# MoE outputs weighted as they leave PSUM and summed in DRAM by an accumulating scatter, instead of stored as pairs and summed at the end

## The reference, cut to what matters

```python
x = x + concat([y_ssd, y_hgrn]) @ w_out            # the residual rows
h = rmsnorm(x, norm_ffn_w)
p_group = softmax(h @ router_group)                # 4 groups, the best one is taken
g_w = max(p_group)
top_w, top_i = top_k(softmax(logits of that group), 2)   # 2 of its 4 experts
top_w = top_w / sum(top_w)
c = g_w * top_w                                    # two gates for each token
for each of 16 experts e:                          # D 1024, expert width 256
    hid = silu(h @ w_gate[e]) * (h @ w_up[e])
    y  += c[e] * (hid @ w_down[e])
out = rmsnorm(x + y, final_norm_w)
```

## Time and profile before

| | us |
|---|---|
| median of 3 runs | 499.08 (498.66 to 503.92) |
| the profiled execution: device time | 501.04 |
| its span, first to last instruction | 499.3 |
| PE busy | 447.5 (90%) |
| DVE / ACT / POOL busy | 339.0 / 273.1 / 145.5 |
| moved by DMA | 92.99 MB, mean 186 GB/s |
| chain that ended last | PE 75%, DVE 14%, ACT 5%, DMA 3%, issue 2% |

### The profile page before, as it was taken

One profiled execution on the slowest core, in us unless ns is written; L12 is line 12 of the kernel. 1 busy time (PEld: TensorE's weight loads), 2 busy tenths in 40 slices (PEclk: granted clock), 3 DMA queues, 4 the chain that ended last, 5 costly groups with the idle time before them and its releaser, 6 DMA issues.

```text
span 499.3 us, 7114 instructions
## 1 busy us (share of the span) xinstructions
PE 447.5 (90%) x2783; PEld 391.5 (78%) x2783; DVE 339.0 (68%) x504; ACT 273.1 (55%) x440; POOL 145.5 (29%) x110
## 2 busy tenths in 40 slices
PE   2799999999999999999899988899999999999500
PEld 2378888899898899999899987788888888888400
DVE  3424688772769685798866238577787787777357
ACT  6725273623543243145445325479899899888422
POOL 3520000000000000111510211557887887865100
PEclk9899999999999979999999998999999999999955
DMA  8541222222202012206087921569999999984185
GB/s 298 222 159 61 109 84 86 84 85 85 84 1 85 18 68 85 85 1 253 1 328 265 341 85 47 168 251 377 354 388 379 357 378 379 358 319 161 45 310 204
DMA packets 20768, 92.99 MB, mean 186 GB/s; under 512 B 4812, under 2 KB 7032, under 8 KB 12280
## 3 DMA queue, kind: packets, MB, share of 16 engines
q1 hardware_dynamic: 13992, 81.95, 43.7%
q0 software_dynamic: 4096, 8.41, 5.0%
q10 hardware_dynamic: 2640, 2.11, 1.3%
HBM read 87.21 MB, written 11.54 MB: 198 GB/s over the span
## 4 chain that ended last, share of the span: by engine, by line
PE 75%; DVE 14%; ACT 5%; DMA 3%; issue 2%; SPq 0%; DVEq 0%; POOLq 0%; ACTq 0%
PE bank L1520 45%; PE bank L1799 6%; PE bank L1801 6%; PE bank L1800 6%; PE bank L1787 3%; DVE arena L1477 2%; DVE actl L992 1%; DMA X<-in_x_dram 1%; DMA arena<-pairs_dram 1%; PE bank L1504 1%; PE bank L1661 1%; PE bank L1677 1%; DVE wl L998 1%; DMA pairs_dram<-arena 1%; PE bank L1827 1%
## 5 line engine op out<-in xcount | busy, mean ns | idle before, releaser
L1520 PE MATMUL bank<-wh,acth 128*128 128x256 f32 x320 | 93.2, 291 | 3.3 <-DVE actl L992 1.9
L1520 PE MATMUL bank<-wl,acth 128*128 128x256 f32 x320 | 91.7, 287 | 0.0
L1520 PE MATMUL bank<-wh,actl 128*128 128x256 f32 x320 | 91.6, 286 | 0.0
L1520 PEld LDWEIGHTS bank<-wh,acth 128*128 128x128 f32 x320 | 62.7, 196 | 3.7 <-issue 3.7
L634 POOL TENSOR_TENSOR wl<-raw,wh 128x1024 fp32r<-128x1024 f32 x21 | 50.5, 2427 | 47.4 <-ACT wh L870 47.4
L580 POOL TENSOR_TENSOR arena<-arena,bc 128x512 f32<-128x512 f32 x4 | 6.6, 1656 | 194.0 <-DVE arena L1072 194.0
L1520 PEld LDWEIGHTS bank<-wl,acth 128*128 128x128 f32 x320 | 62.7, 196 | 0.0
L1520 PEld LDWEIGHTS bank<-wh,actl 128*128 128x128 f32 x320 | 62.5, 195 | 0.0
L1799 PE MATMUL bank<-wh,acth 128*128 128x512 f32 x128 | 51.9, 406 | 1.8 <-DVE actl L1396 1.7
L1520 PE MATMUL bank<-acth,wh 128*128 128x512 f32 x128 | 50.4, 394 | 0.0
L1801 PE MATMUL bank<-wh,actl 128*128 128x512 f32 x128 | 50.2, 392 | 0.0
(11 more groups left out here) (312 smaller groups left out, 1009.2 us busy)
## 6 DMA issues: line engine op xcount, KB each, us to landing
raw<-in_w_units_dram SPq DMA_DIRECT2D x18, 1024.0 KB, 4.8
raw<-in_w_gate_up_dram SPq DMA_DIRECT2D x17, 1024.0 KB, 10.9
arena<-in_w_down_dram SPq DMA_DIRECT2D x16, 1024.0 KB
arena<-in_w_gate_up_dram SPq DMA_DIRECT2D x15, 1024.0 KB
arena<-pairs_dram SPq DMA_DIRECT2D x8, 512.0 KB, 7.2
X<-in_x_dram SPq DMA_DIRECT2D x4, 512.0 KB, 5.6
arena<-in_x_dram SPq DMA_DIRECT2D x1, 2048.0 KB, 10.9
h_dram<-X ACTq DMA_DIRECT2D x4, 512.0 KB, 3.6
```

The lines of the kernel that those rows point to most:

```text
L1520: ins = te.matmul(acc_ap, a, b, start=(j == 0), stop=(j == n - 1))
```

## The change

**What it does.** (1) The two gates are computed right after the tables, not after the loop; their products with the chosen-expert masks (`gv`) are taken through eight PE products with a float32 copy (`wide`, made by ACT) of the one-hot slots, which gives each slot's gate, `gsl` (`slot_gates`); 26 `keep_warm` become 14, then `slot_gates`, then 6. (2) ACT's copies of an expert's output from PSUM multiply by `gsl`. (3) The residual rows are also stored to DRAM, as `sums_dram`, one store of 512 KB beside each of the four of `h2_dram`. (4) The scatter adds to `sums_dram` (`compute_op=ALU.add`) by the same indices as the gather; `six` and half of `vals` go. (5) Experts run in the order PERM (0, 4, 8, 12, 1, 5, ...), so experts of one group are four apart. (6) The tail loads four tiles of `sums_dram` into `xres` in place of eight; `add_pairs` goes. (7) The `lgf` copies move ahead of the sum of squares and the last `weigh_rows`. (8) At expert 1 ACT takes the tokens between the two halves of `round_a(1)`, and DVE takes tokens 1 before the rest of a(1).

```diff
+        PERM = [(e % G) * EG + e // G for e in range(NE)]
-            for tt in range(TT):
-                for c in range(2):
-                    sp.dma_start(pairs[tt][:, c, :], pairs_dram[c * T + tt * P:c * T + (tt + 1) * P, :])\
-                        .then_inc(pair_in[tt][c], 16)
+            for tt in range(TT):
+                sp.dma_start(xres[:, tt, :], sums_dram[tt * P:(tt + 1) * P, :]).then_inc(sum_in[tt], 16)
...
@@ scatter
-                gp.indirect_dma_start(pairs_dram, bass.IndirectOffsetOnAxis(ap=six[0:CAP, e:e + 1], axis=0),
-                                      ysb[j][0:CAP, :], None, bounds_check=2 * T - 1, oob_is_err=False)\
-                    .then_inc(sca_out[j], 16)
+                gp.indirect_dma_start(sums_dram, bass.IndirectOffsetOnAxis(ap=gix[0:CAP, PERM[e]:PERM[e] + 1], axis=0),
+                                      ysb[j][0:CAP, :], None, bounds_check=T - 1, oob_is_err=False,
+                                      compute_op=ALU.add).then_inc(sca_out[j], 16)
...
+            pool.wait_ge(res_st, 16 * (n_front - n_in))
             pool_round(0, 0, True)
@@ store_rows
                 act.dma_start(h2_dram[:, c].rearrange("(t p) n -> p t n", p=P), X[:, :, c]).then_inc(h2_st, 16)
+                act.dma_start(sums_dram[:, c].rearrange("(t p) n -> p t n", p=P), xres[:, :, c]).then_inc(res_st, 16)
@@ act_expert
-                sc.activation(ysb[e % YB][:, 0:512], bank[5][:, :], ACT.Copy).then_inc(y0_ok, 1)
+                sc.activation(ysb[e % YB][:, 0:512], bank[5][:, :], ACT.Copy,
+                              scale=gsl[:, PERM[e]:PERM[e] + 1]).then_inc(y0_ok, 1)
@@ act_round
+                act.wait_ge(tab_q, r * 2 + 2)
+                sc.activation(wide, onehot, ACT.Copy).then_inc(wide_ok, 1)
+                act.wait_ge(gs_mm, r + 1)
+                sc.activation(gsl, bank[7][:, 64:64 + NE], ACT.Copy).then_inc(gsl_ok, 1)
+                act.wait_ge(gsl_ok, r + 1)
                 round_tokens(base, 0)
                 act.wait_ge(gu_a, base + 1)
-                round_a(r, 1)
+                round_a(r, 1, (0,))
                 round_tokens(base + 1, 1)
+                round_a(r, 1, (1,))
...
@@ DVE, after the tables and `rounds` (moved from behind the loop; gv is new)
+            ch.link(ve.tensor_reduce(r1[:, 6], r4[:, 1], AX_X, ALU.add))
+            ch.link(ve.tensor_scalar(r1[:, 7], r1[:, 4], 1.0, None, ALU.add))
+            ch.link(ve.tensor_tensor(r1[:, 7], r1[:, 7], r1[:, 6], ALU.mult))
+            ch.link(ve.reciprocal(r1[:, 8], r1[:, 7]))
+            ch.link(ve.tensor_tensor(r1[:, 9], r1[:, 8], r1[:, 4], ALU.mult))
+            ve.tensor_tensor(gv, r16[:, 1:3], r1[:, 8:10].unsqueeze(3).broadcast_to([P, 2, TT, NE]),
+                             ALU.mult).then_inc(gv_ok, 1)
...
@@ PE
+            def slot_gates(r):
+                pe.wait_ge(gv_ok, 1)
+                pe.wait_ge(tab_ok, r + 1)
+                pe.wait_ge(wide_ok, r + 1)
+                for c in range(2):
+                    for tt in range(TT):
+                        ins = te.matmul(bank[7][:, 64:64 + NE], wide[:, c, tt, :], gv[:, c, tt],
+                                        start=(c == 0 and tt == 0), stop=(c == 1 and tt == TT - 1))
+                ins.then_inc(gs_mm, 1)
@@ pe_round
                 find_all(r)
-                keep_warm(26)
+                keep_warm(14)
+                slot_gates(r)
+                keep_warm(6)
                 turn_tokens(r, base, 0)
```

More of the change, by code:

```diff
@@ L234, in trunk @@
         onehot = gate[:, 0, :].bitcast(F16).rearrange("p (c t s) -> p c t s", c=2, t=TT)
-        vals = part(2 * TT * NE).bitcast(F16).rearrange("p (c t i e) -> p c t i e", c=2, t=TT, i=2)
+        vals = part(TT * NE).bitcast(F16).rearrange("p (c t e) -> p c t e", c=2, t=TT)
         sil = part(FE)
@@ L239, in trunk @@
         iotai = part(P).bitcast(I32)
-        tokc = part(2 * TT).rearrange("p (t i) -> p t i", i=2)
+        tokc = part(TT)
         prio = part(EG)
@@ L248, in trunk @@
         ss = part(TT * D // UC).rearrange("p (t u) -> p t u", t=TT)
-        r4 = part(12 * TT * 4).rearrange("p (i t n) -> p i t n", i=12, t=TT)
+        r4 = part(5 * TT * 4).rearrange("p (i t n) -> p i t n", i=5, t=TT)
         r1 = part(12 * TT).rearrange("p (i t) -> p i t", i=12)
@@ L256, in trunk @@
         gix = part(NE).bitcast(I32)
-        six = part(NE).bitcast(I32)
+        gv = part(2 * TT * NE).rearrange("p (c t e) -> p c t e", c=2, t=TT)
+        gsl = part(NE)
+        wide = ysb[2].rearrange("p (c t s) -> p c t s", c=2, t=TT)
         rnd = part(4)
         rounds = part(1).bitcast(I32)
-        pairs = [arena[:, a:a + 2 * D].rearrange("p (c n) -> p c n", c=2) for a in (0, 2 * D, 8 * D, 10 * D)]
         assert ofs[0] <= 22528
@@ L395, in trunk @@
         pool_tick = sem("pool_tick")
-        res_ok = sem("res_ok")
         fsd_ok = sem("fsd_ok")
@@ L401, in trunk @@
         sca_out = [sem(f"sca_out{j}") for j in range(YB)]
-        pair_in = [[sem(f"pair_in{t}_{c}") for c in range(2)] for t in range(TT)]
+        sum_in = [sem(f"sum_in{t}") for t in range(TT)]
+        res_st = sem("res_st")
+        gv_ok = sem("gv_ok")
+        wide_ok = sem("wide_ok")
+        gs_mm = sem("gs_mm")
+        gsl_ok = sem("gsl_ok")
         h2_dram = nc.dram_tensor("h2_dram", (T, HROW), F32, kind="Internal").ap()
-        pairs_dram = nc.dram_tensor("pairs_dram", (2 * T, D), F32, kind="Internal").ap()
+        sums_dram = nc.dram_tensor("sums_dram", (T, D), F32, kind="Internal").ap()
         AHEAD_DVE = ((gl_ok, 2), (hl_ok, 1), (hid_ok, 1))
@@ L948, in act_expert @@
                 y_free(act, r, e, first_round)
-                sc.activation(ysb[e % YB][:, 0:512], bank[5][:, :], ACT.Copy).then_inc(y0_ok, 1)
+                sc.activation(ysb[e % YB][:, 0:512], bank[5][:, :], ACT.Copy,
+                              scale=gsl[:, PERM[e]:PERM[e] + 1]).then_inc(y0_ok, 1)
                 act.wait_ge(dn, step * 2 + 4)
-                sc.activation(ysb[e % YB][:, 512:1024], bank[6][:, :], ACT.Copy).then_inc(y1_ok, 1)
+                sc.activation(ysb[e % YB][:, 512:1024], bank[6][:, :], ACT.Copy,
+                              scale=gsl[:, PERM[e]:PERM[e] + 1]).then_inc(y1_ok, 1)
             def act_round(r, base, first_round=False):
@@ L974, in _ @@
             for tt in range(TT):
-                act.wait_ge(res_ok, tt + 1)
+                act.wait_ge(sum_in[tt], 16)
                 ch.link(sc.activation(X[:, tt, :], xres[:, tt, :], ACT.Square, accum_out=st[:, 0, tt:tt + 1]))
@@ L1308, in _ @@
             turned_low(len(halves_out) - 1)
+            dve.wait_ge(moe_mem, 1)
+            for tp in range(2):
+                dve.wait_ge(rk_ok, 4 * (n_front - n_in) - 2 + 2 * tp)
+                ve.tensor_copy(lgf[:, tp * UC:(tp + 1) * UC], bank[6 + tp][0:2 * NL, 0:UC]).then_inc(lg_c, 1)
             dve.wait_ge(sq_ok, 1)
@@ L1312, in _ @@
             dve.wait_ge(std_ok, TT + 3)
-            dve.wait_ge(moe_mem, 1)
             ve.reciprocal(rs[:, :, 0], st[:, 5, 0:TT]).then_inc(rs_ok, 1)
-            for tp in range(2):
-                dve.wait_ge(rk_ok, 4 * (n_front - n_in) - 2 + 2 * tp)
-                ve.tensor_copy(lgf[:, tp * UC:(tp + 1) * UC], bank[6 + tp][0:2 * NL, 0:UC]).then_inc(lg_c, 1)
             dve.wait_ge(lg_mm, 1)
@@ L1379, in tables @@
                 ve.tensor_scalar(gix, bank[7][:, 0:NE], float(NO_SLOT), None, ALU.add).then_inc(tab_ok, 1)
-                ve.tensor_scalar(six, bank[7][:, NE:2 * NE], float(NO_SLOT), None, ALU.add).then_inc(tab_ok, 1)
             find_all()
@@ L1390, in _ @@
             ve.tensor_copy(rounds, rnd[:, 1:2]).then_inc(routed, 1)
+            dve.wait_ge(ge_ok, 1)
+            ch.link(ve.tensor_reduce(r1[:, 6], r4[:, 1], AX_X, ALU.add))
+            dve.wait_ge(e2_ok, 1)
+            ch.link(ve.tensor_scalar(r1[:, 7], r1[:, 4], 1.0, None, ALU.add))
[4 more added lines that the diff above has]
+                             ALU.mult).then_inc(gv_ok, 1)
             def rest_tokens(step, b):
@@ L1449, in dve_round @@
                 rest_tokens(base, 0)
+                rest_tokens(base + 1, 1)
                 c = slice(UNIT // 2, UNIT)
@@ L1463, in _ @@
             later_rounds(dve, dve_round)
[L1465 to L1471, removed]
-            dve.wait_ge(bc3_in, 16)
[L1474 to L1481, removed]
+            dve.wait_ge(bc3_in, 16)
             def final_norm(tt):
@@ L1487, in final_norm @@
                                         ALU.mult).then_inc(fin_ok, 1)
[L1489 to L1493, removed]
+            for tt in range(TT):
+                final_norm(tt)
         @block.tensor
@@ L1775, in find_all @@
                     for tt in range(TT):
-                        ins = te.matmul(bank[7][:, 0:2 * NE], onehot[:, c, tt, :],
-                                        vals[:, c, tt].rearrange("p i e -> p (i e)"),
+                        ins = te.matmul(bank[7][:, 0:NE], onehot[:, c, tt, :], vals[:, c, tt],
```

(2 more changed lines are left out.)

23 lines of the change are left out of this document (8 added, 15 removed).

## The result

| | before | after |
|---|---|---|
| median of 13 runs each | 500.41 us | 504.78 us |
| ratio of the runs, 95% interval | | 1.0053 (1.0027 to 1.0079) |
| span of the profiled execution | 499.3 us | 499.5 us |

The change made the kernel slower by half a per cent, about 2.7 us. The two medians lie further apart than that; runs of one kernel spread over some 6 to 8 us, and the ratio with its interval is the figure to go by.

A forecast was written before the change was run, and what follows sets the result against it. PE was taken as the bound up to about 455 us, with no DMA reserve left at the end. 499.3 - 9.2 - 0.2 - 1.4 + 15.6 - 0.5 + 1.2 = 504.8, given as 504.5 us, range 489 to 512.

The forecast's parts named there:

- What bounded the kernel: Expert loop before the change: bound by PE to about 455 us, transfers' lead eaten at 1.35 us an expert.
- rival B: Expert loop: the scatter's added reads cost under 0.2 us an expert, giving 489 us, up to 491; chance 0.22.
- The tail: After the last PSUM copy: four tiles loaded for eight and no adds of pairs, 9.2 us saved, certain within 1.
- the last scatter: End of the chain, alone: seven extra reads add about 1.2 us to 4.2 us.
- Start of the loop: Routing and expert 1, before the loop's steady part: 0.2 us and 1.4 us gained.
- Expert 1: Start of the loop: tokens taken first remove PE's wait of 1.69 us; gain 1.1 to 1.7 us, 1.4 taken.
- The add: Scatter in the expert loop: extra reads cost 1.2 us an expert, thirteen times, 15.6 us, less about 0.5.
- The lead: Loads in the expert loop: issued some 20 us ahead, lead eaten by about 390 us, landing times stopping at about 22.
- rival C: Expert loop: the added reads cost part, 0.3 to 0.8 us an expert, total 491 to 500 us; chance 0.12.
- The signs: Loop and tail: lag growing 2.5 us an expert, ACT waits, PE share below 0.85, pace about 12 us, tail 20.5.
- rival D: Expert loop: reads cost more than a copy, or PE's clock falls; 508 to 520 us; chance 0.16.
- The Trainium skill's rule: Scatter with add: two read descriptors a chunk, 1.93 times a plain copy, making the add's term 14.5 us, not 15.6.

The follow-up runs named there:

- the second profiled execution: The changed kernel measured once more, unaltered, against the kernel before: 505.04 us, ratio 1.0059 (1.0024 to 1.0093).
- the spread kernel: The changed kernel with neighbouring slots dealt to partitions 7 apart: 492.49 us, ratio 0.983 to the kernel before; on another chip 491.24 us, 0.9793.

## Why the prediction was right, point by point

**What bounded the kernel: right.** The step from three loads' landing times to a kernel bound by PE with no reserve left in DMA is what decided the sign. The strip and the busy shares alone would have given the forecast of rival B, 489 us: all that the tail gives.

**The tail: right.** 9.2 us less for loads and adds and 1.2 more for the last scatter, 8.0 together; measured 8.3. ACT did set the pace of the tiles (squares start at 489.19, 490.58, 492.00, 493.39: 1.4 us each, forecast 1.5), and the last scatter got 1.6 us longer, of which POOL's longer descriptor writing, 0.5 us, was not foreseen.

**Start of the loop: right in sum.** Without the 1.46 us that the execution was ahead anyway, the loop began 1.4 us sooner; forecast 1.6. The gather landed 1.1 us sooner than in the earlier trace rows, but PE turned tokens at 313.21, that is 0.15 us later on the same count: the filler took all of it and not three quarters. Expert 1 gave 1.5 us, forecast 1.4. Its product comes with no wait for DVE's a(1), as said: the rows of after that answer to the earlier trace rows are

```profile
319.33 1.07 ACT L925 ACTIVATE acth<-bank 128x512 fp32r<-128x512 f32 x2
320.29 1.06 ACT L873 ACTIVATE wh<-raw 128x1024 fp32r<-128x1024 f32 x1
321.38 1.63 DVE L1470 TENSOR_TENSOR wl<-raw,wh 128x1024 fp32r<-128x1024 f32 x1
```

and DVE's split is over at 323.01, before PE's seventh product at 323.53 wants it. PE's first product has no idle time before it that the profile lays to a wait:

```profile
322.07 0.47 PE L1805 MATMUL bank<-wh,acth 128*128 128x512 f32 x1
```

**The add: right mechanism, mis-sized term.** Forecast 15.6 us less 0.5; measured 11.1, and no 0.5 was found (the chain behind the last `load_b` was 0.2 us longer and not 0.5 shorter, so the kernel before had no such slack). The price of a row was right: 0.18 taken, 0.19 measured. What failed is the next factor, the pace: I let each expert cost 7 x 0.18, 1.2 us, all through. In the saturated stretch it was more: `load_a` landed at 364.3, 376.3, 388.8 and 401.6 us, 12.4 an expert for 10.6 in the same stretch of before (landings 363.7 and 395.6), so 1.8 more. Later it was less: at 435.5 (408.5 + 27.0) and 458.7 us (431.3 + 27.4), two experts apart, so 11.6, where before went at 10.9, so 0.7 more. Over thirteen experts that is 0.85 and not 1.2. Why an expert costs DMA more than forecast at first and less later stays open. Later is when the mean DMA share is 0.90 in place of 1.00, so some engines rest, and a row may be cheaper where fewer compete; no run separates this.

**The lead.** I said that the lag would stop at 22 us, since that was all the lead there was. It stopped at 27. The lead is a count of experts, 22.1 / 9.42 = 2.35 of them, and when the pace falls to 11.6 us it lasts longer: 2.35 x 11.6 = 27. So the loop turned near 397 us, as ACT's first long wait shows, and not at 390.

**The total: near by luck.** 504.5 was said (the terms add up to 504.8) and 504.78 measured. But the forecast difference was 504.5 - 499.08 = 5.4 us, and the ratio gives 2.7: the add's term was 4 us too large, and the median of before, 499.08 over three runs, came out at 500.41 over thirteen. The likeliest outcome by the prediction, slower by more than 1% (0.44), did not come either; 0.5% is under what it counted as a difference. In rival C's sum the base is 499.3 - 9.2 - 0.2 - 1.4 = 488.5 and not 489.3, so it comes to 497.9 and not 498.5; the forecast does not use it.

**The signs.** Of those named for being right, the growing lag, ACT's waits (16.6 us in seven, all for `load_b`), the pace of about 12 us, the tail and expert 1 came. PE's share in 400 to 450 us was to fall below 0.85 and was 0.89. And a granted clock under 1.00 in the loop was named as a sign of rival D: it came, 0.94 in that stretch, without D's cost, so it was no sign that could tell the two apart.

**The Trainium skill's rule, Collectives: The Full Stack, section The bandwidth ceiling.** Two read descriptors for a chunk, a factor of 1.93. From 330 to 440 us the software queue took these shares (packets, MB, share), first in the kernel without the add, then in after:

```profile
q0 software_dynamic: 2889, 5.66, 14.9%
```

```profile
q0 software_dynamic: 2752, 5.39, 19.8%
```

By the megabyte 2.63 and 3.67%, so 1.40 times for gathers and scatters together. If a gather and a scatter of the same rows cost alike, the scatter costs 1.8 times its plain price. Over the whole execution the same assumption gives more: 5.0% of 16 engines for 499.3 us is 399 engine-us, so 200 for the plain scatters, and the add put 192 on them, 1.96 times. The traces agree with the rule, whose number lies between the two.

**Rival D, the clock.** It was seen, and cost the time nothing that shows. From the loop's first load to the end of the last PSUM copy PE was busy 146.1 us in after and 141.0 in before, with 684 records of products in each: 5.1 of the 11.3 us that this stretch lost are slower products, the rest waits. From 410 to 420 us the granted clock of after is 0.83, from 440 to 450 us 0.89, means over stretches that lay partly at the lower level, 1.2 GHz. It fell after PE had stood still:

```profile
413.26 0.47 PE L1805 MATMUL bank<-wh,acth 128*128 128x512 f32 x1 [2.03 <-DVE wl L1419]
...
416.02 0.63 PE L1806 MATMUL bank<-wl,acth 128*128 128x512 f32 x1
```

Such a product takes 0.39 us before the wait. But PE worked slower in a time in which it would have waited for loads: the chain that ended last has no piece of PE from 373.98 to 463.61 us; three loads `load_b` alone are 75.8 us of it. And the second profiled execution, with a clock of 0.97 in 400 to 450 us where this one has 0.94, took as long for the loop, 137.9 us.

## What to carry to other kernels

Take the times to landing of the same load, a few iterations apart, before a transfer is made dearer or added: here a lag that grew told that DMA was full, though PE was busy 100% of the time, and how long the lead would still last. An add in a scatter is not free because no engine makes it; here it cost nearly as much again as the scatter, 10 to 12 us of 500 at a full DMA, and nothing that can be told once the rows were spread. Where an indirect transfer has unfilled slots at its end, deal the slots over all partitions, which here turned a change that lost 0.5% into one that gains 1.7 to 2.1%.

## What the runs showed of the hardware that was not expected

A scatter of 112 slots with the add keeps POOL busy for 1.46 to 1.54 us, the plain one for 0.93 to 0.97 (single ones, late in the loop, took up to 2.34 with it and up to 1.88 without), though its packets in the profile are as many (4096 over the run in both). The add's second read shows neither in the packets nor in the bytes of the DMA queues (8.42 and 8.41 MB) nor in the bytes read from DRAM (85.12 MB in both), only in the time they took, 7.4% for 5.0%: a byte count does not find it.

An ACT copy of 128x512 from PSUM whose scale is a column in SBUF took 0.68 us, with a constant scale 0.59; the prediction had counted nothing for it. It stands twice an expert in ACT's 44 of 50 busy us, and PE, busy 50.00 of 50 us in the spread kernel, did not wait for it.
